# One TensorE loop from zero in the expert phase, all remainders of the up units on VectorE, and no drain at the end of an item

## The reference, cut to what matters

```
probs = softmax(t @ router_w + router_b); top_p, top_i = top_k(probs, 2)
order = argsort(top_i.reshape(-1));  xs = t[order // 2]            # 2048 rows, sorted by expert
hid = silu(ragged_dot(xs, w1, sizes)) * ragged_dot(xs, w3, sizes)  # w1, w3: 1024 x 3584 for each expert
y   = ragged_dot(hid, w2, sizes) * top_p[order]                    # w2: 3584 x 1024
out = zeros.at[order // 2].add(y)
```

## Time and profile before

| | |
|---|---|
| median of the runs | 5752.77 us |
| the profiled execution: time, span | 5747.08 us, 5745.2 us |
| granted TensorE clock, mean over the span | 0.965 |
| TensorE matmul busy | 5331.3 us (93%) |
| VectorE busy | 2440.8 us (42%) |
| ScalarE busy | 1811.5 us (32%) |
| GpSimd busy | 1822.2 us (32%) |
| `rest13` on GpSimd | 170 of 6283 ns, 1066.4 us |
| `rest13` on VectorE | 170 of 2806 ns, 477.0 us |
| `rest2` on VectorE | 168 of 2340 ns, 390.5 us |

### The profile page before, as it was taken

The page is one execution under the profiler, slowest core; times in us unless marked ns, Lnnn a source line. Parts: engine busy times, 40 slices in busy tenths (PEclk is TensorE's granted clock), DMA queues, the critical chain, the costliest instruction groups (busy, mean ns, idle before and its releaser), DMA issues. The chain is left out here.

```text
span 5745.2 us, 71348 instructions
## 1 busy us (share of the span) xinstructions
PE 5331.3 (93%) x29660; PEld 4454.9 (78%) x29661; DVE 2440.8 (42%) x2324; ACT 1811.5 (32%) x1596; POOL 1822.2 (32%) x499
## 2 busy tenths in 40 slices
PE   7998999999999899999986989989999899998995
PEld 4676667678888667667766988979899898897984
DVE  6334257343525434423323423333554247733356
ACT  3113121132221212312123333333453336643344
POOL 1310111134444141111114242515443326651443
PEclk8999999999999999999998999999999999999997
DMA  4211124324636421111216545555685459965578
GB/s 169 73 52 36 50 78 115 111 85 121 183 99 173 131 69 42 54 37 49 71 63 223 194 161 192 174 169 190 228 284 195 160 188 312 331 205 169 192 232 292
DMA packets 810508, 854.87 MB, mean 149 GB/s; under 512 B 19250, under 2 KB 732082, under 8 KB 809906
## 3 DMA queue, kind: packets, MB, share of 16 engines
q1 hardware_dynamic: 802274, 820.18, 44.3%
q0 software_dynamic: 4608, 16.78, 0.8%
q10 hardware_dynamic: 3408, 14.68, 0.7%
HBM read 793.90 MB, written 57.67 MB: 148 GB/s over the span
## 5 line engine op out<-in xcount | busy, mean ns | idle before, releaser
L2216 POOL TENSOR_TENSOR e_w_lo<-e_raw,e_w_hi 128x2048 fp32r<-128x2048 f32 x170 | 1066.4, 6283 | 1565.5 <-ACT e_w_hi L2154 1565.5
L258 PE MATMUL banks<-e_x_hi,e_w_hi 128*128 128x256 f32 x3584 | 1023.1, 285 | 81.9 <-issue 70.7
L258 PE MATMUL banks<-h_hi,w_hi 128*128 128x512 f32 x2432 | 994.0, 409 | 57.0 <-DVE h_lo L737 22.2
L259 PE MATMUL banks<-e_x_lo,e_w_hi 128*128 128x256 f32 x3584 | 1022.6, 285 | 16.8 <-issue 16.8
L260 PE MATMUL banks<-e_x_hi,e_w_lo 128*128 128x256 f32 x3584 | 1021.4, 285 | 0.0
L259 PE MATMUL banks<-h_lo,w_hi 128*128 128x512 f32 x2432 | 955.8, 393 | 0.0
L260 PE MATMUL banks<-h_hi,w_lo 128*128 128x512 f32 x2432 | 955.4, 393 | 0.0
L2154 ACT ACTIVATE e_w_hi<-e_raw 128x2048 fp32r<-128x2048 f32 x340 | 648.2, 1911 | 535.4 <-PE banks L260 523.9
L258 PEld LDWEIGHTS banks<-e_x_hi,e_w_hi 128*128 128x128 f32 x3584 | 692.9, 193 | 85.2 <-issue 72.8
L259 PEld LDWEIGHTS banks<-e_x_lo,e_w_hi 128*128 128x128 f32 x3584 | 692.7, 193 | 18.6 <-issue 18.6
L260 PEld LDWEIGHTS banks<-e_x_hi,e_w_lo 128*128 128x128 f32 x3584 | 692.7, 193 | 0.0
(11 more groups left out here) (310 smaller groups left out, 7465.9 us busy)
## 6 DMA issues: line engine op xcount, KB each, us to landing
e_raw<-in_moe_w_dram SPq DMA_DIRECT2D x510, 1024.0 KB, 5.1
w_raw<-in_ffn_w_dram SPq DMA_DIRECT2D x120, 512.0 KB, 3.9
w_raw<-in_w_in_dram SPq DMA_DIRECT2D x108, 512.0 KB, 4.2
f_ada_raw<-in_ada_w_dram SPq DMA_DIRECT2D x48, 512.0 KB, 5.0
g_ada_raw<-in_ada_w_dram SPq DMA_DIRECT2D x32, 512.0 KB, 4.2
e_io<-row_scratch SPq DMA_DIRECT2D x13, 1024.0 KB, 6.3
x_scratch<-x_res SPq DMA_DIRECT2D x24, 512.0 KB, 2.8
row_scratch<-stage SPq DMA_DIRECT2D x24, 512.0 KB, 2.6
```

What stands on the lines that cost most here:

```text
L258: pe.matmul(out, wh, rh, start=first, stop=False)
L259: pe.matmul(out, wh, rl, start=False, stop=False)
L2216: eng.tensor_tensor(flat(w_lo[u]), flat(raw[n % RING]), flat(w_hi[u]).bitcast(F32), ALU.subtract).then_inc(lo_sem[u % 2], 1)
```

## The change

In `expert_phase`:

- VectorE makes the remainders of all four up units; GpSimd has no program left in this phase. Each of the four units has a semaphore of its own in place of two shared ones.
- `up_narrow` is one hardware loop over all seven iterations. Its first iteration turns an old `act_t[1]` into bank 7 (two transposes whose result nobody reads), so `hid_turned` counts one more for each item, and the wait for `y_in` moves into `turn_hidden`.
- The drain and `y_done` go; ScalarE waits for the count of the last down unit (`mm_done`) instead.

```
-        lo_sem = (s.lo1, s.lo3)
+        lo_sem = (s.lo_u0, s.lo_u1, s.lo_u2, s.lo_u3)
...
                 if n < UP:
-                    sp.wait_ge(lo_sem[n % 2], 2 * NFG * item + 2 * (n // 4) + n % 4 // 2 + 3)
+                    sp.wait_ge(lo_sem[n % 4], NFG * item + n // 4 + 3)
...
-                    act.wait_ge(s.y_done, item + 1)
+                    act.wait_ge(s.mm_done, UNITS * item + UNITS + 4)
...
-        @block.gpsimd
-        def _(pool):
-
-            pool.sem_inc(s.lo3, 2)
-            for h in range(2):
-                rest13(pool, 0, 0, 2 * h + 1)
-            n_items = field(pool, 0, 3, MAX_ITEMS)
-            with pool.Fori(0, MAX_ITEMS) as item:
-                with pool.If(item < n_items):
-                    for i in range(1, NFG):
-                        for h in range(2):
-                            rest13(pool, item, i, 2 * h + 1)
-                    for h in range(2):
-                        rest13(pool, item + 1, 0, 2 * h + 1)
...
                 pe.wait_ge(s.hid_lo, g + 1)
+                if h == 1:
+                    pe.wait_ge(s.y_in, item + 1)
                 for f in range(2):
...
             def up_narrow(item):
-                for u in range(4):
-                    up_unit(item, 0, u)
-                pe.wait_ge(s.y_in, item + 1)
-                turn_hidden(item, 0, 0)
-                with pe.Fori(1, NFG) as i:
+                with pe.Fori(0, NFG) as i:
                     up_unit(item, i, 0)
                     up_unit(item, i, 1)
                     turn_hidden(item, i - 1, 1)
...
-                        pe.sem_inc(s.hid_turned, 2 * NFG)
+                        pe.sem_inc(s.hid_turned, 2 * NFG + 1)
...
                         down(item, ITEM)
-                    pe.drain().then_inc(s.y_done, 1)
...
                         for i in range(1, NFG - 1):
                             gated(item, i, 0, 2 * P)
                             turned(item, i - 1, 1)
                             rest13(dve, item, i + 1, 0)
+                            rest13(dve, item, i + 1, 1)
                             gated(item, i, 1, 2 * P)
                             turned(item, i, 0)
                             rest13(dve, item, i + 1, 2)
+                            rest13(dve, item, i + 1, 3)
...
-                            for h in range(2):
-                                hidden(item, i, h)
-                                rest13(dve, item, i + 1, 2 * h)
+                            hidden(item, i, 0)
+                            rest13(dve, item, i + 1, 0)
+                            rest13(dve, item, i + 1, 1)
+                            hidden(item, i, 1)
+                            rest13(dve, item, i + 1, 2)
+                            rest13(dve, item, i + 1, 3)
...
-                    for h in range(2):
-                        rest13(dve, item + 1, 0, 2 * h)
+                    for u in range(4):
+                        rest13(dve, item + 1, 0, u)
```

More of the change, by code:

```diff
@@ L2087, in field @@
         return eng.value_load(m.items[0:1, ds(4 * item + col, 1)], min_val=0, max_val=hi)
-    with phase(nc, "x_in", "raw0", "raw1", "raw2", "raw3", "raw4", "raw5", "hi_ready", "lo1", "lo3", "lo2", "mm_done", "turned", "x_hi", "x_lo",
-               "silu", "hid", "hid_turned", "hid_hi", "hid_lo", "y_done", "y_in", "y_stored", "closed") as (block, s):
+    with phase(nc, "x_in", "raw0", "raw1", "raw2", "raw3", "raw4", "raw5", "hi_ready", "lo_u0", "lo_u1", "lo_u2", "lo_u3", "lo2", "mm_done", "turned", "x_hi", "x_lo",
+               "silu", "hid", "hid_turned", "hid_hi", "hid_lo", "y_in", "y_stored", "closed") as (block, s):
         raw_sem = (s.raw0, s.raw1, s.raw2, s.raw3, s.raw4, s.raw5)
-        lo_sem = (s.lo1, s.lo3)
+        lo_sem = (s.lo_u0, s.lo_u1, s.lo_u2, s.lo_u3)
         @block.sync
@@ L2215, in rest13 @@
             eng.wait_ge(s.hi_ready, UNITS * item + n + 1)
-            eng.tensor_tensor(flat(w_lo[u]), flat(raw[n % RING]), flat(w_hi[u]).bitcast(F32), ALU.subtract).then_inc(lo_sem[u % 2], 1)
-        @block.gpsimd
-        def _(pool):
-            pool.sem_inc(s.lo3, 2)
-            for h in range(2):
-                rest13(pool, 0, 0, 2 * h + 1)
-            n_items = field(pool, 0, 3, MAX_ITEMS)
-            with pool.Fori(0, MAX_ITEMS) as item:
-                with pool.If(item < n_items):
-                    for i in range(1, NFG):
-                        for h in range(2):
-                            rest13(pool, item, i, 2 * h + 1)
-                    for h in range(2):
-                        rest13(pool, item + 1, 0, 2 * h + 1)
+            eng.tensor_tensor(flat(w_lo[u]), flat(raw[n % RING]), flat(w_hi[u]).bitcast(F32), ALU.subtract).then_inc(lo_sem[u], 1)
         @block.tensor
@@ L2255, in up @@
                             pe.wait_ge(s.hid, 2 * (NFG * item + i) + h + 1)
-                        pe.wait_ge(lo_sem[q], 2 * (NFG * item + i) + h + 3)
+                        pe.wait_ge(lo_sem[u], NFG * item + i + 3)
                         hi, lo = by_k(w_hi[u]), by_k(w_lo[u])
@@ L2335, in _ @@
                         down(item, ITEM)
-                    pe.drain().then_inc(s.y_done, 1)
         @block.vector
         def _(dve):
-            dve.sem_inc(s.lo1, 2)
+            for u in range(4):
+                dve.sem_inc(lo_sem[u], 2)
             dve.sem_inc(s.lo2, 2)
@@ L2370, in turned @@
             def turned(item, i, h):
-                dve.wait_ge(s.hid_turned, 2 * (NFG * item + i) + h + 1)
+                dve.wait_ge(s.hid_turned, (2 * NFG + 1) * item + 2 * i + h + 2)
                 split(item, i, h, m.ps[:, 6 + h, 0:2 * P], P)
@@ L2380, in _ @@
             x_rest(1)
-            for h in range(2):
-                rest13(dve, 0, 0, 2 * h)
+            for u in range(4):
+                rest13(dve, 0, 0, u)
             n_items = field(dve, 0, 3, MAX_ITEMS)
@@ L2389, in _ @@
                         rest13(dve, item, 1, 0)
+                        rest13(dve, item, 1, 1)
                         gated(item, 0, 1, 2 * P)
@@ L2392, in _ @@
                         rest13(dve, item, 1, 2)
+                        rest13(dve, item, 1, 3)
                         for i in range(1, NFG - 1):
```

## The result

The changed kernel takes 5611.86 us, median of four runs (5606.67 to 5612.57), beside 5752.06 us (5751.0 to 5755.46) of the kernel before on the same chip: ratio 0.9753, 95% interval 0.9736 to 0.977, 140 us less. The forecast was 5617 us in a range of 5600 to 5690. The profiled execution took 5612.09 us, its span is 5610.2 us, the mean granted clock 0.974.

The account below looks back on a forecast made before the run. TensorE, busy 93% of the span, was taken as the bound, idling mostly on instruction fetch between items. Terms 96.5 + 33 + 4.4 + 3 + 3 - 5 = 135 us off 5747.1 gave 5612, plus 5.7: 5617 us, range 5600 to 5690.

Parts of the forecast that it names:

- The gaps come from the sequencer, and the loop can be made to fit: TensorE's gaps between items are instruction fetch stalls; the change takes wide items from nine packets to eight, which its memory keeps.
- the first rival: TensorE's memory keeps seven packets, or a far branch always stalls: only 68 us saved, 5685 us, chance 0.16.
- w-w: Step from a wide item to a wide one, five times: gap of 14.2 us goes to about 0.1; 96.5 us saved.
- the second stall: TensorE's further wait of 2.42 us, four matmuls into a wide item behind a wide one; forecast to go.
- w-n: Step from a wide item to a narrow one, three times: 11.1 us saved each, 33 in all (27 to 38).
- DMA floor of 12.6 us: Narrow up iteration: loading four units of 1.05 MB at 334 GB/s at most needs 12.6 us; 12.2 taken.
- n-n: Step from a narrow item to a narrow one, once (item 9): 4.4 us saved (2 to 8).
- the floor of 133.5 us: Least time for item 9, narrow behind narrow, from its DMA queue being busy 96.8% of 137.9 us.
- n-w: Step from a narrow item to a wide one, twice: earlier start, 1.5 us saved each, 3 in all.
- First item: The first item's stall of 3.7 us shortens since the packet boundary moves: 3 us saved (0 to 4).
- What is dropped from the memory: Narrow and wide code don't both fit: no stall if least recently used goes, a loss if oldest goes; -5 us taken.
- Slower, by VectorE's 4.42 us: Rival: arriving loads, not GpSimd, make VectorE's remainder in narrow items take 4.42 us; 5850 us, chance 0.03.

Follow-up runs that it names:

- e2: Kernel before with only the narrow up loop made a single hardware loop; drain and GpSimd's remainders stay: 5666.48 us, ratio 0.9855.
- e4: Changed kernel with the first narrow up iteration written out again: 5684.12 us, ratio 0.9886.
- e5: Changed kernel with 100 never-run instructions (50 transposes) behind the narrow down part: 5610.46 us, ratio 0.9755.
- e6: Changed kernel with 150 never-run instructions (75 transposes) behind the narrow down part: 5655.97 us, ratio 0.9835.
- e7: Changed kernel with the first six iterations of VectorE's wide branch rolled into a hardware loop: 5589.97 us, ratio 0.9719.
- e10: Changed kernel with GpSimd making every second up remainder again: 5642.0 us, ratio 0.9811.
- e9: Changed kernel with the drain and its count `y_done` back: 5639.5 us, ratio 0.9806.
- e3: Kernel before with all up remainders on VectorE and GpSimd's program gone; drain and written-out iteration stay: 5733.4 us, ratio 0.9971.
- e8: Kernel before with all up remainders on VectorE and VectorE's wide branch rolled into a loop; drain and written-out iteration stay: 5726.89 us, ratio 0.9955.
- e1: Kernel before without the drain alone; ScalarE waits for the count of the last down unit: 5697.88 us, ratio 0.9909.

## Why the prediction was right, point by point

*The gaps come from the sequencer, and the loop can be made to fit.* Right, and shown from three sides: e2 makes the loop fit and nothing else, e4 undoes it alone, e5 and e6 put the edge between 100 and 150 dead instructions. The memory keeps eight packets of 256, as the power of two and the Trainium skill (Runtime: NRT & Kernel Launch, Instruction fetch mechanics) had it, and the first rival (seven, or a far branch always stalls) fell. Its price of 5685 is met by e4's 5684.12, but by errors that cancel: the gaps w-w are 6.3 us and not 9.9, the second stall, which I had gone, is 6.1, so the five items w-w save 20 us and not 34; the narrow items save more than I had given them.

*w-w, 96.5 us.* Measured 93. Items 2 to 4 saved 18.6 to 18.9 against 19.3 forecast; 7 and 11 still miss once.

*w-n, 33 us.* Measured 31.4, but by two errors that cancel. The step that failed is the DMA floor of 12.6 us in an iteration: a share of 0.98 was read as capacity, and the same engines moved 363 GB/s later. The steady half iteration is TensorE's 5.97 us. What I left out is VectorE's program. With one more remainder in each half iteration, of narrow and of wide items, it no longer fits its own memory, and each narrow item pays 2.4 to 4.3 us at its start (e7). I had costed VectorE's instructions, not their code.

*n-n, 4.4 us.* Measured 6.2; the floor of 133.5 us was too high for the same reason, the item takes 131.8 here and 127.5 in e7.

*n-w, 3 us.* Measured 4.4: start after 1.6 us as forecast, and the low clock of 3.4 us gone.

*First item, 3 us.* 3.8.

*What is dropped from the memory, -5.* Neither of the two orders is right (below). The cost was two branch stalls of 3.6 us under a lead of 4: some 3 us at the starts of items 7 and 11, which the 93 us above already hold.

*Slower, by VectorE's 4.42 us.* Fell: in the changed kernel the up remainders on VectorE average 2285 ns while 363 GB/s of loads arrive. GpSimd was the cause: in e10, where it works again, those of item 5 average 3995 ns, against 2283 in the up part of that item in the changed kernel.

*The sum.* 135 us from the profiled execution, and the two profiled spans differ by 135.0. The 5 us between the forecast of 5617 and the median of 5611.86 are the 5.7 us that I added because the profiled execution before lay that far under its median; the one after does not (5612.09).

## What to carry to other kernels

Where an engine's idle time is "issue" and sits at a hardware loop's branch, count the loop's instructions with both sides of its conditions: dead code costs nothing until it needs one packet more than the memory keeps, and then a refetch of everything, 45 us here. Work moved to another engine brings its code along; look at the instruction queues for packets inside the loop, on every engine, before and after. Two edits that shorten the same gap don't add up, so undo each by itself before pricing it.

## What the runs showed of the hardware that was not expected

A new packet doesn't take the place of the oldest one or of the least recently used one. For the loop of e2 and e9 (both 6 0 0 0 3 4 2 3 0 4 2 3 packets by item) the oldest-first rule gives 6 0 0 0 1 8 0 1 4 4 0 1 and least recently used 6 0 0 0 3 2 0 3 0 2 0 3. The counts are those of a ring of eight places. A packet that is loaded ahead goes into the place behind the one that calls it, and the target of a branch that misses into the place behind that. A narrow item so overwrites the first packets of the wide code, the wide item after it reloads all that follow and at last the top, and the item after that misses the top. The places of the stalls agree: in e2 and e9 the branch to the top stalls behind items 6 and 10 alone. Oldest-first would have it stall behind items 5 and 8, and by least recently used no branch back to the top would stall. The rule also gives all twelve counts of the kernel before, 7 9 9 9 5 5 9 5 0 5 9 5, but so do the other two, so it rests on the small loop. It was fitted to that loop and not tested on one made for it.

What a miss costs goes with the data that move meanwhile. The branch to the top takes 5.4 to 6.0 us behind a drain (before, e2, e3, e8 and e9) and 3.3 to 3.9 without one (e1, e4 to e7, e10, the changed kernel). Without the drain it comes while the raw buffers are full and nothing is loaded, with it when the loads of the next item have begun (the last number is GB/s; the changed kernel behind item 6, the kernel before behind item 1):

```profile
4409.20:4412.80 3.60, 3.60 (x18) 2.98 (x17) 2.29 (x1) 0.62 (x1) 0.00 (x0) 1.00 0.02 5
...
3319.70:3325.40 5.70, 0.00 (x0) 0.00 (x0) 0.00 (x0) 4.89 (x3) 3.94 (x1) 0.86 0.75 259
```

The packet's own transfer takes 1.2 and 1.1 us there; it begins 1.0 us into the first branch and 3.3 us into the second. All stalled branches of TensorE in the items of the twelve traces fall into four groups: 3.3 to 3.9 us at 4 to 7 GB/s, 4.9 to 6.0 at 246 to 282, 5.8 to 6.3 at 316 to 328, and 6.4 to 7.1 at 338 to 359. The second group also has the branches into the wide code of e1, e4 and e6, which have no drain in front. So the drain need not slow the fetch; it puts the branch where the loads are. As no run changed the loads alone, this is a reading and not shown.
